# Transposes, causal heads and dilated groups of a two-block model, rearranged over the slots of TensorE's weight stream

## What is computed

```python
# block 1, causal part: 8 heads of 64; q and k are RMS-normalised per head
qh = rmsnorm(to_heads(q_b), q_norm_w[l]); kh = rmsnorm(to_heads(k_b), k_norm_w[l])
y_ch = chunked_relpos_attention(qh, kh, to_heads(v_b), rel_bias[l])   # softmax(q k + bias) v
# block 1, stick-breaking part: 4 heads, around the end of the causal part
y_sb = stick_breaking_attention(q_a, k_a, v_a)
# block 2, 12 heads in 3 groups (dilation 1, 4, 16); for each of 4 head positions the
# three groups are mixed by a softmax over their log sums
y_b = dilated_mixture_attention(q, k, v)
```

## Time and profile before

| | |
|---|---|
| median of 3 executions | 695.27 us (695.19 to 695.75) |
| profiled execution | 695.06 us, its span 693.3 us |
| PE busy | 686.9 us, 99% of the span |
| DVE, ACT, POOL busy | 461.5, 373.8, 35.7 us |
| chain that ended last | PE 98% |
| granted TensorE clock | full in all 40 slices of the span |
| HBM read | 122.34 MB, 178 GB/s over the span |

### The profile page before, as it was taken

How to read it: one execution, slowest core, us unless ns; L and a number is a source line. 1 busy time by engine, 2 the same in 40 slices (tenths; PEclk the granted TensorE clock), 3 DMA queues, 4 the chain that set the end, 5 groups by cost and what they waited for, 6 DMA issues and landing times.

```text
span 693.3 us, 12179 instructions
## 1 busy us (share of the span) xinstructions
PE 686.9 (99%) x5132; PEld 646.4 (93%) x5132; DVE 461.5 (67%) x738; ACT 373.8 (54%) x567; POOL 35.7 (5%) x33
## 2 busy tenths in 40 slices
PE   9999999999999999999999999999999999999996
PEld 8889999999999998889988898999999999998885
DVE  5975776976666664665674568558698888887422
ACT  6865764754444443456365475444566555555322
POOL 0400131200000000011000000000020000000000
PEclk9999999999999999999999999999999999999999
DMA  9953334355555566446364333434637555556501
GB/s 333 359 191 122 122 121 185 126 207 195 196 190 184 182 207 219 181 160 233 132 241 166 140 127 124 177 127 177 244 147 249 182 183 182 184 186 239 181 1 61
DMA packets 20102, 124.17 MB, mean 179 GB/s; under 512 B 2256, under 2 KB 3536, under 8 KB 5840
## 3 DMA queue, kind: packets, MB, share of 16 engines
q1 hardware_dynamic: 17856, 120.02, 48.2%
q10 hardware_dynamic: 2192, 3.38, 1.5%
HBM read 122.34 MB, written 1.05 MB: 178 GB/s over the span
## 4 chain that ended last, share of the span: by engine, by line
PE 98%; issue 1%; ACT 0%; POOL 0%; POOLq 0%; DVE 0%; ACTq 0%
PE pm L323 52%; PE psc L323 33%; PE ptr L323 8%; PE po L323 3%; PE ptr L326 1%; PE po L326 0%; PE psc L326 0%; PE pm L1684 0%; PE psc L1684 0%; ACT yo L329 0%; ACT sq L332 0%; POOLq L181 0%; POOL rcol L335 0%; POOL ones L360 0%; DVE rms L338 0%
## 5 line engine op out<-in xcount | busy, mean ns | idle before, releaser
L335 DVE TENSOR_TENSOR wl<-raw,wh 128x1024 fp32r<-128x1024 f32 (+1 forms) x226 | 270.1, 1209 | 41.2 <-ACT wh L332 29.4
L332 ACT ACTIVATE wh<-raw 128x1024 fp32r<-128x1024 f32 (+1 forms) x226 | 228.6, 1036 | 52.8 <-PE psc L323 34.6
L323 PE MATMUL pm<-xh,wh 128*128 128x256 f32 x560 | 158.4, 283 | 0.0
L323 PE MATMUL pm<-xl,wh 128*128 128x256 f32 x560 | 156.4, 279 | 0.0
L323 PE MATMUL pm<-xh,wl 128*128 128x256 f32 x560 | 156.3, 279 | 0.0
L323 PEld LDWEIGHTS pm<-xh,wh 128*128 128x128 f32 x560 | 105.3, 188 | 2.8 <-issue 2.5
L323 PEld LDWEIGHTS pm<-xl,wh 128*128 128x128 f32 x560 | 105.3, 188 | 0.0
L323 PEld LDWEIGHTS pm<-xh,wl 128*128 128x128 f32 x560 | 105.2, 188 | 0.0
L323 PE MATMUL psc<-xh,wh 128*128 128x256 f32 x304 | 85.0, 280 | 0.0
L323 PE MATMUL psc<-xl,wh 128*128 128x256 f32 x304 | 84.9, 279 | 0.0
L323 PE MATMUL psc<-xh,wl 128*128 128x256 f32 x304 | 84.8, 279 | 0.0
(11 more groups left out here) (300 smaller groups left out, 1228.1 us busy)
## 6 DMA issues: line engine op xcount, KB each, us to landing
raw<-in_w_dram SPq DMA_DIRECT2D x109, 1024.0 KB, 4.8
early<-in_w_dram SPq DMA_DIRECT2D x2, 1024.0 KB, 11.9
raw<-in_w_dram SPq DMA_DIRECT2D x2, 512.0 KB, 6.8
bias<-in_rel_dram ACTq DMA_DIRECT2D x1, 1024.0 KB, 7.9
xa<-in_xt_dram SPq DMA_DIRECT2D x3, 256.0 KB, 6.6
out_dram<-yo SPq DMA_DIRECT2D x3, 256.0 KB, 2.3
raw<-in_w_dram ACTq DMA_DIRECT2D x2, 256.0 KB, 4.8
raw<-in_w_dram SPq DMA_DIRECT2D x2, 256.0 KB, 5.2
```

The source lines that it names most:

```text
L323: return lambda e: e.matmul(dst, lhs, rhs, start=start, stop=stop, skip_group_check=True)
L332: return lambda e: e.activation(dst, src, kind, **kw)
L335: return lambda e: e.tensor_tensor(dst, a, b, op)
```

## The change

The two pairs of keys are turned in one go in slot 9, into T and M[1], and both of queries in slot 10, into T and M[2]. Of the causal heads both of a pair pass each step in the same slot: max and exp one slot behind the scores, transposes two behind, copies three and values four behind, so that PE's steps fall into every second slot; the second head's transposes use S[1] (the last one's M[0]). In the dilated part the first pair's scores of groups 0 and 1 stand in one slot, with T and O as further banks, and the second pair's transposes of groups 0 and 1.

```diff
-        def head_turn(name, src, i):
...
+        def head_turn(name, src, other):
+            banks = tok[name, "banks"] = [T, other]
+            for i, bank in enumerate(banks):
+                after = bank.claim() + [tok[name, "n"], tok["cf"]]
...
+        when(VB + 1, 60, lambda: head_turn("k", kvs, M[1]))
+        when(VB + 2, 60, lambda: head_turn("q", qvs, M[2]))
         for i in range(2):
-            when(VB + 1 + 2 * i, 60, lambda i=i: head_turn("k", kvs, i))
-            when(VB + 2 + 2 * i, 10, lambda i=i: head_keep("k", kbt, i, qkw[:, 0:1]))
-            when(VB + 2 + 2 * i, 60, lambda i=i: head_turn("q", qvs, i))
-            when(VB + 3 + 2 * i, 10, lambda i=i: head_keep("q", qbt, i, None))
+            when(VB + 2, 10 + i, lambda i=i: head_keep("k", kbt, i, qkw[:, 0:1]))
+            when(VB + 3, 10 + i, lambda i=i: head_keep("q", qbt, i, None))
...
+        def ch_bank(h):
+            return T if h % 2 == 0 else S[1] if h < 7 else M[0]
...
-        for h in range(8):
-            if h % 2 == 0:
-                when(SC + h, 60, lambda h=h: ch_scores(h // 2))
-            when(SC + h + 1, 30, lambda h=h: ch_max(h))
-            when(SC + h + 1, 60, lambda h=h: ch_exp(h))
-            when(SC + h + 2, 60, lambda h=h: ch_turn(h))
-            when(SC + h + 3, 10, lambda h=h: ch_keep(h))
-            when(SC + h + 3, 60, lambda h=h: ch_values(h))
+        for p in range(4):
+            b = SC + 2 * p
+            when(b, 60, lambda p=p: ch_scores(p))
+            for h in (2 * p, 2 * p + 1):
+                when(b + 1, 30, lambda h=h: ch_max(h))
+                when(b + 1, 60, lambda h=h: ch_exp(h))
+                when(b + 2, 61, lambda h=h: ch_turn(h))
+                when(b + 3, 10, lambda h=h: ch_keep(h))
+                when(b + 4, 59, lambda h=h: ch_values(h))
...
+        def dl_score_bank(pair, g, i):
+            return S[(2 * g + i) % 3] if pair else (S + [T, O] + S)[2 * g + i]
...
-        def dl_bank(pair, i):
+        def dl_bank(pair, i, g):
+            if pair and g == 1:
+                return S[1 + i]
             return T if i == 0 else S[0] if pair else O
...
             for g in range(3):
-                when(b + g, 60, lambda p=pair, g=g: dl_scores(p, g))
-                when(b + g + 1, 30, lambda p=pair, g=g: dl_soft(p, g))
+                at = b + (g if pair else g // 2)
+                when(at, 60, lambda p=pair, g=g: dl_scores(p, g))
+                when(at + 1, 30, lambda p=pair, g=g: dl_soft(p, g))
...
                 for g in range(3):
-                    when(b + 5 + 2 * g, 60, lambda p=pair, i=i, g=g: dl_turn(p, i, g))
-                    when(b + 6 + 2 * g, 10 + i, lambda p=pair, i=i, g=g: dl_keep(p, i, g))
+                    at = b + 5 + (2 * (g // 2) if pair else 2 * g)
+                    when(at, 60, lambda p=pair, i=i, g=g: dl_turn(p, i, g))
+                    when(at + 1, 10 + i, lambda p=pair, i=i, g=g: dl_keep(p, i, g))
```

More of the change, by code:

```diff
@@ L788, in head_scale @@
                 tok[name, "n"] = dve.do(tt(v, v, f, ALU.mult), tok[name, "f", tb], tok[name, "raw", tb])
-        def head_turn(name, src, i):
[L791 to L799, removed]
+        def head_turn(name, src, other):
+            banks = tok[name, "banks"] = [T, other]
+            for i, bank in enumerate(banks):
+                after = bank.claim() + [tok[name, "n"], tok["cf"]]
+                for pj in range(2):
+                    for tb in range(2):
+                        c0 = (2 * i + pj) * P
+                        f = tr(bank.ap[:, pj * 256 + tb * P:pj * 256 + tb * P + P], src[:, tb, c0:c0 + P])
+                        if pj and tb:
+                            tok[name, "t"] = tok[name, "t", i] = pe.do(f)
+                        else:
+                            pe.quiet(f, *after)
         def head_keep(name, dst, i, scale):
-            d = dst[:, 2 * i:2 * i + 2, :]
+            d, bank = dst[:, 2 * i:2 * i + 2, :], tok[name, "banks"][i]
             if scale is None:
-                t = act.do(func(d, pairs(T.ap), ACT.Copy), tok[name, "t"])
+                t = act.do(func(d, pairs(bank.ap), ACT.Copy), tok[name, "t", i])
             else:
-                t = act.do(scaled(d, pairs(T.ap), scale), tok[name, "t"], tok["qkw"])
+                t = act.do(scaled(d, pairs(bank.ap), scale), tok[name, "t", i], tok["qkw"])
             tok[name, "ready", i] = t
-            T.release(t)
+            bank.release(t)
         when(QB + 2, 10, lambda: head_norm("k", (M[0], M[1]), kvs))
@@ L875, in ch_exp @@
                                            accum_out=den[:, d:d + 1]), tok["cm", h], *used)
+        def ch_bank(h):
+            return T if h % 2 == 0 else S[1] if h < 7 else M[0]
         def ch_turn(h):
-            after = T.claim() + [tok["ce", h]]
+            bank = ch_bank(h)
+            after = bank.claim() + [tok["ce", h]]
             for i in range(3):
-                f = tr(T.ap[:, i * P:i * P + P], pb[:, h % 2, i * P:i * P + P])
+                f = tr(bank.ap[:, i * P:i * P + P], pb[:, h % 2, i * P:i * P + P])
                 if i == 2:
@@ L887, in ch_keep @@
             used = [tok["cp", h - 3]] if h >= 3 else []
-            d = ptb[:, h % 3, :]
+            d, bank = ptb[:, h % 3, :], ch_bank(h)
             if h % 2:
-                t = act.do(func(d, T.ap[:, 0:384], ACT.Copy), tok["ct", h], *used)
+                t = act.do(func(d, bank.ap[:, 0:384], ACT.Copy), tok["ct", h], *used)
             else:
-                t = dve.do(lambda e: e.tensor_copy(d, T.ap[:, 0:384]), tok["ct", h], *used)
+                t = dve.do(lambda e: e.tensor_copy(d, bank.ap[:, 0:384]), tok["ct", h], *used)
             tok["ck", h] = t
-            T.release(t)
+            bank.release(t)
         def ch_values(h):
@@ L1470, in build @@
         when(V2 + 6, 10, lambda: tokens_out("w2b", (M[2], ), 256, v2s, 512))
+        def dl_score_bank(pair, g, i):
+            return S[(2 * g + i) % 3] if pair else (S + [T, O] + S)[2 * g + i]
         def dl_scores(pair, g):
             after = [tok["q2", "ready", g], tok["k2", "ready", g]]
-            for i in range(2):
-                after += S[(2 * g + i) % 3].claim()
+            banks = [dl_score_bank(pair, g, i) for i in range(2)]
+            for bank in banks:
+                after += bank.claim()
             j = 2 * g + pair
@@ L1480, in dl_scores @@
                     lo, c = 64 * i, qs.start
-                    f = mm(S[(2 * g + i) % 3].ap[:, c:c + ks.stop], q2t[lo:lo + 64, j, qs],
+                    f = mm(banks[i].ap[:, c:c + ks.stop], q2t[lo:lo + 64, j, qs],
                            k2t[lo:lo + 64, j, ks], c == 0, c > 0)
@@ L1490, in dl_soft @@
             for i in range(2):
-                bank = S[(2 * g + i) % 3]
+                bank = dl_score_bank(pair, g, i)
                 used = [tok["dt", i, g]] if pair else []
@@ L1520, in dl_divide @@
                     r, tok["de", i])
-        def dl_bank(pair, i):
+        def dl_bank(pair, i, g):
+            if pair and g == 1:
+                return S[1 + i]
             return T if i == 0 else S[0] if pair else O
         def dl_turn(pair, i, g):
-            bank = dl_bank(pair, i)
+            bank = dl_bank(pair, i, g)
             after = bank.claim() + [tok["dq", i]]
@@ L1536, in dl_keep @@
             used = [tok["dp"]] if pair else []
-            dst, bank = pt2[:, i, g, :], dl_bank(pair, i)
+            dst, bank = pt2[:, i, g, :], dl_bank(pair, i, g)
             if g == 1:
```

## The result

The changed kernel takes 697.11 us (median of 7 executions, 696.86 to 697.9) and the kernel before 695.32 on the same chip: ratio 1.0031, 95% interval 1.0022 to 1.004. It is slower, within the range, 0.2 us above the forecast. Its executions fall into two groups: four of seven took 696.9 to 697.1 us, three took 697.9. The granted clock, averaged over each execution, goes with the groups: 0.998 to 0.999 in the four, 0.996 to 0.997 in the three. The profiled one took 697.89, its span is 696.1 us and its clock 0.996, so it belongs to the upper group.

What follows compares the result with a forecast made beforehand. PE, busy 99% of the span, was taken to bound the kernel. Wait +1.94, heads and causal work +0.16, dilated part -0.41 gave +1.7 us: 696.9 us, range 696.3 to 697.5 alone, 694.8 to 698.0 for 8 in 10.

Steps and rivals of the forecast that it cites:

- The wait: Slot 18, T its stream's start: keep(5) on ACT delays square and ch_max(6), so PE waits before stick-breaking scores, +1.94 us.
- Heads and causal work without the wait: Slots 9 to 21: PE's own time for turning keys and queries in one go and pairing causal heads, +0.16 us.
- sb_after: Triangular products in slot 21, needing DVE's last low part: about 0.5 us of slack, up to 0.5 us more if it fails.
- the exit of scores into transposes: Three causal score islands now left into transposes: between 0 and -0.10 us each, taken as 0.
- nearest in type: Reason for taking 0 for those three islands: f32 transposes resemble the f32 stream more than the bf16 mask products.
- The second wait: Rival: slack before the triangular products used up, or ACT later in slot 18, +0.5 to +1.5 us; chance 0.11.
- The dilated part: Slots 125 to 142: one score island less -0.40 us, two transpose islands in one -0.01, together -0.41 us.
- The clock: Rival: PE's pace falls after the 2 us gap in slot 18, half of 4.8 us lost, 699.3 us; chance 0.04.
- the forecast alone: The main case without rivals: 696.9 us, range 696.3 to 697.5; chance 0.65.
- the whole range: Range for 8 in 10, with no wait and part of the second wait included: 694.8 to 698.0 us.
- Interruptions cost a switch: Rival: each of six vanished islands saves 0.3 to 0.4 us, some -2.1 beside the wait, 694.9 us; chance 0.05.

Runs made afterwards that it cites:

- run 2: Changed kernel with the group norm's steps ahead of keep(4) and ch_max(6), ch_max(7) ahead of the low part: 694.59 us, ratio 0.9993.
- Run 7: Kernel before with only the dilated edit, scores and transposes of two groups together: 694.51 us, ratio 0.9992.
- run 5: Kernel before with only the keys and queries turned in one go each: 695.1 us, ratio 0.9999.
- run 6: Kernel before with only the causal heads by pairs: 698.47 us, ratio 1.0042.
- run 9: The changed kernel itself measured once more, nothing altered: 697.97 us, ratio 1.0037 to the kernel before.
- experiment 3: Changed kernel with 8 extra f32 matmuls (16 instructions, result unused) on PE in slot 18's wait: 696.43 us, ratio 1.002.

## Why the prediction was right, point by point

**The wait** was the step that decided, and it holds to 0.1 us. Forecast from T: keep(5) +0.28, square over +1.76, ch_max(6) over +4.87, scores +4.92. Measured with T = 67.68: +0.28, +1.74 (69.42), +4.86 (72.54), +4.97. The difference is the signal from DVE to PE, 0.11 and not 0.05. PE would have been ready at T + 2.98 (run 2), so the wait costs 1.99 us; the forecast was 1.94.

**Heads and causal work without the wait.** Forecast +0.16. At the first stream matmul behind sb_after the profiled execution stands 3.39 us behind that of before (91.62 against 88.23), and it had begun the weight stream 0.12 earlier, so 3.51 us were added. Less 1.99 of wait and 1.52 of clock this leaves 0.00, inside the -0.15 to +0.2. The term that was taken too high is the exit of scores into transposes, three times. Its row:

```profile
49.87 0.55 PE L326 MATMUL ptr<-cfs,pb 128*128 128x128 f32 x3
50.25 0.49 PE L326 MATMUL psc<-cfs,pb 128*128 128x128 f32 x3
```

Three transposes take 0.38 from start to start where they take 0.33 elsewhere (three at 0.11), so 0.05 and not 0.11 stays of the exit: -0.15 in all. It lay midway between the two bounds; "nearest in type" had picked one end. The Trainium skill (TensorEngine Tiling (Array Packing), Key Properties) says that a change of the tiling mode drains the engine and names no exception for what follows; the 0.05 agrees that something is paid, though half of what the stream pays.

**sb_after.** I said about 0.5 us of slack; DVE's last low part is over at 88.25 (87.56 + 0.69) and PE comes at 89.30: 1.0 us. The second wait did not happen.

```profile
87.56 0.69 DVE L335 TENSOR_TENSOR spl<-sp,sph 128x512 fp32r<-128x512 f32 x1
...
89.30 0.48 PE L323 MATMUL psc<-sph,trir 128*128 128x512 f32 x1
```

**The dilated part.** Forecast -0.41. From the first island to the first transposes of this part PE needs 16.74 us (395.06 to 411.80), and 17.22 before (391.72 to 408.94): -0.48. The missing entry and exit are -0.40 of it; where the other 0.08 lie was not traced. Run 7 gives -0.67 by its median, and its interval takes in both.

**The clock** was the rival that I held for nearly excluded (0.04, at 2.4 us). By the times and mean clocks it happens in 3 of 7 and 4 of 5 executions of the changed kernel; the two that were profiled lost 1.52 and 1.55 us by it, and the groups lie 0.9 and 1.2 us apart. The forecast left it out, and here luck had a share: the median is right because four of the first seven executions did not show it. In the second sample the median is 697.97, outside the 696.3 to 697.5 that the forecast alone allowed and at the edge of the whole range: a median of two groups depends on how many of each were drawn. The step that failed is the weight of this rival. I had written that the trace has no gap to judge by, and that is a reason for a larger chance, not for 0.04.

**Interruptions cost a switch** is not borne out: two islands less of full-array work in run 5 gave 0.1 us or nothing, and the whole change without its wait (run 2) gained 0.4 us where this rival asks for some 2.1.

**What stays open.** In which executions the clock falls, and whether the lower group is quite free of it: with the fill the kernel takes 696.43, and the profiled execution less its 1.52 us of clock would be at 696.4 too, but the lower group stands at 696.8 to 697.1. In run 6, whose profile is one of the lower group, the clock after the wait is full, but the start of the weight stream alone differs by up to 0.3 us from one profiled execution to another, which is as much as the difference sought.

## What to carry to other kernels

When two engines work through fixed orders, look at which instruction stands first in the slot and what it waits for: a copy put ahead of a chain of 4.2 us (copy, square, reduce, low part, max) delayed the chain by its own wait, and one changed priority took 2 us back. When a step makes an otherwise gapless PE wait for some 2 us, price the slower clock behind the wait as well, and if the wait can't be removed, filling it with idle matmuls keeps the pace. Merging neighbouring islands of 64-row matmuls pays about 0.4 us each, merging islands of full-array work nothing that could be measured here.

## What the runs showed of the hardware

- The granted clock can fall to the lower of its two levels (1.2 and 2.4 GHz) behind a PE wait of only 1.9 us in a kernel that otherwise keeps PE busy, and it does so in some executions of the same program and not in others. Behind 0.6 us no execution of eleven shows it in its time or its mean clock (0.998 or more), behind 3.4 us all five do (slower than the wait explains, 0.994 to 0.996). The fall can come with the first work behind the gap (clock 0.60 from 72.6 us on) or 1.6 us later (run 9). The Trainium skill (TensorE: Matmul & The Clock Gate, Why this matters for your kernels) warns of idle gaps between bursts that are longer than this one. The traces differ from it: 1.9 us were enough in seven of twelve executions.
- The granted clock on record can read full where the pace is half. The 22 matmuls at the start come 0.21 us apart where the table by windows gives a clock of 1.00; the same instruction comes 0.11 apart in the fill of experiment 3 (16 in 1.95 us). Read the pace as well.
- Going from 64-row matmuls to f32 transposes costs 0.05 us on the first transpose, half of the 0.11 that the f32 stream pays behind the same scores.
- From the end of a DVE instruction to PE's start behind it are 0.11 us (72.54 to 72.65); ACT starts 0.04 behind the same one (72.58).
